# Projecting the prompt's queries in transposed form, and moving their token factors into the group norm's epsilon

## What is computed

```
h = rmsnorm(x);  u, q, k, v, g = split(h @ w_in)            # 1024 -> 5 x 512
pool_out = pool_mix(u)                                       # trailing means, a 128x128 product per group
qh, kh = rope(q), rope(k) * 128 ** -0.5                      # 4 heads of 128
# retention, chunks of 128 tokens, per head, gamma a constant of the head
scores = (qc @ kc.T) * decay_mat                             # gamma^(i-j) for i >= j
o = scores @ vc + (qc * gamma^(i+1)) @ s
s = s * gamma^128 + (kc * gamma^(127-j)).T @ vc
o = (o - mean(o)) * rsqrt(var(o) + GN_EPS) * gn_g            # group norm over a head's 128 values
x = x + concat(pool_out, silu(g) * o) @ w_out
```

## Time and profile before

| what | value |
|---|---|
| three runs | 836.44, 837.12 (median), 838.64 us |
| the profiled execution | 837.1 us |
| its span on the core | 835.1 us |
| mean granted TensorE clock | 0.995 of full speed |
| PE busy | 814.2 us, 97% of the span |
| DVE busy | 599.4 us, 72% |
| ACT busy | 483.6 us, 58% |
| POOL busy | 315.4 us, 38% |

### The profile page before, as it was taken

How to read it: one execution, slowest core, us unless ns; L and a number is a source line. 1 busy time by engine, 2 the same in 40 slices (tenths; PEclk the granted TensorE clock), 3 DMA queues, 4 the chain that set the end, 5 groups by cost and what they waited for, 6 DMA issues and landing times.

```text
span 835.1 us, 11973 instructions
## 1 busy us (share of the span) xinstructions
PE 814.2 (97%) x4104; PEld 656.6 (79%) x4104; DVE 599.4 (72%) x957; ACT 483.6 (58%) x824; POOL 315.4 (38%) x205
## 2 busy tenths in 40 slices
PE   9999999999999999999899999999999999999994
PEld 6887788888867888888488788888878578888861
DVE  5444654645689999999744454656647899999986
ACT  5533342612478888887653433353333898888874
POOL 0016991301041345664100199803101423665540
PEclk9999999999999999999999999999999999999998
DMA  9832223223939999998753222322278599999968
GB/s 323 271 109 76 72 57 98 91 70 137 411 128 361 388 355 377 397 368 300 255 185 92 85 76 64 87 64 78 78 263 346 179 417 360 383 378 391 344 219 280
DMA packets 57422, 188.17 MB, mean 225 GB/s; under 512 B 10877, under 2 KB 11645, under 8 KB 49163
## 3 DMA queue, kind: packets, MB, share of 16 engines
q1 hardware_dynamic: 44314, 156.55, 52.2%
q0 software_dynamic: 10368, 23.09, 7.4%
q10 hardware_dynamic: 2688, 7.88, 2.5%
HBM read 173.00 MB, written 29.39 MB: 242 GB/s over the span
## 4 chain that ended last, share of the span: by engine, by line
PE 71%; DVE 16%; DMA 5%; issue 4%; ACT 2%; DVEq 0%; ACTq 0%; POOLq 0%
PE ps L464 14%; PE ps L468 11%; PE ps L467 11%; PE ps L1414 5%; PE ps L1416 5%; PE ps L1415 5%; DVE gul L2110 4%; DVE dnl L2115 3%; PE ps L466 3%; PE ps L1422 2%; DVE hgTl L2126 2%; DMA y_d<-y,rowidx 2%; PE ps L1665 2%; DMA back<-y_d 1%; PE ps L1605 1%
## 5 line engine op out<-in xcount | busy, mean ns | idle before, releaser
L464 PE MATMUL ps<-wh,hT 128*128 128x512 f32 x472 | 189.4, 401 | 0.8 <-DVE wl L2101 0.4
L866 POOL DMA_INDIRECT y_d<-y,rowidx x32 | 116.4, 3638 | 124.1 <-DVE y L2135 124.1
L2110 DVE TENSOR_TENSOR gul<-wgu,eh 128x1024 fp32r<-128x1024 f32 x128 | 150.4, 1215 | 0.5 <-ACT eh L1105 0.5
L468 PE MATMUL ps<-wh,lT 128*128 128x512 f32 x377 | 147.2, 390 | 0.0
L467 PE MATMUL ps<-wl,hT 128*128 128x512 f32 x377 | 147.0, 390 | 0.0
L1105 ACT ACTIVATE eh<-wgu 128x1024 fp32r<-128x1024 f32 x128 | 128.4, 1058 | 3.7 <-PE ps L1416 3.7
L2101 DVE SCALAR_TENSOR_TENSOR wl<-raw,gcol,wh 128x512 fp32r<-128x512 f32 x80 | 75.3, 946 | 67.9 <-ACT wh L1078 67.8
L464 PEld LDWEIGHTS ps<-wh,hT 128*128 128x128 f32 x472 | 88.8, 188 | 18.8 <-issue 1.7
L1414 PE MATMUL ps<-eh,hgTh 128*128 128x512 f32 x240 | 96.4, 401 | 0.4 <-issue 0.4
L1416 PE MATMUL ps<-eh,hgTl 128*128 128x512 f32 x240 | 93.8, 391 | 0.0
L1415 PE MATMUL ps<-gul,hgTh 128*128 128x512 f32 x240 | 93.5, 390 | 0.0
(11 more groups left out here) (259 smaller groups left out, 1555.6 us busy)
## 6 DMA issues: line engine op xcount, KB each, us to landing
wgu<-in_gate_up SPq DMA_DIRECT2D x64, 1024.0 KB, 12.6
wdn<-in_w_down SPq DMA_DIRECT2D x64, 512.0 KB, 12.2
raw<-in_w_in SPq DMA_DIRECT2D x79, 256.0 KB, 2.7
raw<-in_w_out SPq DMA_DIRECT2D x32, 256.0 KB, 3.0
back<-y_d SPq DMA_DIRECT2D x16, 512.0 KB, 5.9
s<-in_state_ret POOLq DMA_DIRECT2D x8, 512.0 KB, 4.3
xn_d<-xf ACTq DMA_DIRECT2D x8, 512.0 KB, 6.2
x_in<-in_x_cols SPq DMA_DIRECT2D x8, 288.0 KB, 5.0
```

The lines of the kernel that those rows point to most:

```text
L464: pe.matmul(out, both, w_h, start=first, stop=False)
L468: return pe.matmul(out, l[:, t * P:(t + 1) * P], w_h, start=False, stop=final)
L866: pool.indirect_dma_start(out=y_d, out_offset=bass.IndirectOffsetOnAxis(ap=rowidx[:, 1, e:e + 1], axis=0), in_=y[s][:, :], in_offset=None, ...
L2110: ve.tensor_tensor(gu_pair(gul, gul3, e, s, p), gu_pair(wgu, wgu3, e, s, p), gu_split(e, p)[:, :].bitcast(F32), ALU.subtract).then_inc(glo, 1)
```

## The change

- For the q block, and the four prompt tiles, the operands change places: a 128-column slice of `wh` or `wl` is stationary and all 512 prompt tokens stream, so a bank then holds one head of q, already transposed (128 dimensions on the partitions, 512 tokens along them). The number of matmuls and their widths stay.
- The bank is copied out without `rstd`. A token's factor, and the decay of its row, scale a whole row of the output, and the group norm takes that out again when its epsilon is divided by the factor's square: `gneps` (a table) times `msq` (the mean square plus epsilon), added to the variance by one more small DVE operation (`gnv`). `q_decay` and `qdT` go; the decay mask becomes one of the key alone.
- POOL rotates q by head (`rotate_turned`): four linked operations over 512 elements, the two in the middle on 64 partitions each, reading one half of the partitions and writing the other. All four heads are rotated before the first k tile.
- `qk_t` transposes only k of the prompt tiles, ACT copies only `kT`. The sample tile keeps the old way; its scores are 64x64.
- `T_AT` and `S_AT` move by one step for tiles 0 and 1.

```diff
-T_AT, S_AT, O_AT = (28, 30, 34, 37), (29, 31, 35, 38), (33, 36, 39)
+T_AT, S_AT, O_AT = (29, 31, 34, 37), (30, 32, 35, 38), (33, 36, 39)
...
+            def rotate_turned(L, h):
+
+                z_there(pool, L, 1, h)
+                v = z[:, h, OFFS["q"], :]
+                cs, sn = c("cosT"), c("sinT")
+                link(pool.tensor_tensor(turnA[:, :], v, cs, ALU.mult))
+                link(pool.tensor_tensor(turnB[0:HALF, :], v[HALF:P, :], sn[HALF:P, :], ALU.mult))
+                link(pool.tensor_tensor(turnB[HALF:P, :], v[0:HALF, :], sn[0:HALF, :], ALU.mult))
+                link(pool.tensor_tensor(v, turnA[:, :], turnB[:, :], ALU.add))
...
-                rotate(L, 0, 0)
-                rotate(L, 1, 0)
+                rotate_turned(L, 0)
+                rotate_turned(L, 1)
                 window(L, 3)
-                rotate(L, 2, 0)
-                for t in range(3):
+                rotate_turned(L, 2)
+                rotate_turned(L, 3)
+                for t in range(LAST):
                     rotate(L, t, 1)
-                for t in (3, LAST):
-                    rotate(L, t, 0)
-                    rotate(L, t, 1)
+                rotate(L, LAST, 0)
+                rotate(L, LAST, 1)
...
-                sc.activation(qT[:, :, :], heads(ps[B_Q][:, :]), ACT.Copy).then_inc(qk_ev, 1)
+                if t == LAST:
+                    sc.activation(qT[:, :, :], heads(ps[B_Q][:, :]), ACT.Copy).then_inc(qk_ev, 1)
...
-                last = tile_mm(pe, ps[m % ZB][:, :], hT[:, k, :], lT[:, k, :], wh[S % SPL][:, :], wl[S % SPL][:, :], t, k == 0, k == KC - 1)
+                if g == 1 and t < LAST:
+                    own = slice(t * P, (t + 1) * P)
+                    last = three(ps[m % ZB][:, :], wh[S % SPL][:, own], wl[S % SPL][:, own], hT[:, k, 0:SEQ], lT[:, k, 0:SEQ], k == 0, k == KC - 1)
+                else:
+                    last = tile_mm(pe, ps[m % ZB][:, :], hT[:, k, :], lT[:, k, :], wh[S % SPL][:, :], wl[S % SPL][:, :], t, k == 0, k == KC - 1)
...
-                for h in range(NH):
-                    pe.transpose(ps[B_Q][:, h * P:(h + 1) * P], zq(t, "q")[:, h * P:(h + 1) * P], ident)
+                if t == LAST:
+                    for h in range(NH):
+                        pe.transpose(ps[B_Q][:, h * P:(h + 1) * P], zq(t, "q")[:, h * P:(h + 1) * P], ident)
...
-                pe.wait_ge(qd_done, T + 1)
...
-                last.then_inc(gn_st, 1)
+                link(last)
+                ve.scalar_tensor_tensor(out=gnv[:, :], in0=c("gneps", 2)[:, int(t == LAST), :], scalar=msq[:, t:t + 1], in1=mv[:, :, 1],
+                                        op0=ALU.mult, op1=ALU.add).then_inc(gn_st, 1)
...
-                    if s - 3 in T_AT:
-                        if s - 3 == T_AT[0]:
-                            ve.wait_ge(upool_st, 32 * (L + 1))
-                        q_decay(L, T_AT.index(s - 3))
...
-                q_decay(L, LAST)
```

More of the change, by code:

```diff
@@ L107, in constant_tables @@
         "decay": np.stack([decay(P), decay(DECS)], 1),
-        "qdec": np.stack([qdecay(P), qdecay(DECS)], 1),
+        "cosT": np.concatenate([np.cos(ang)[:, :LAST]] * 2, 2).transpose(2, 1, 0),
+        "sinT": np.concatenate([np.sin(ang)[:, :LAST], -np.sin(ang)[:, :LAST]], 2).transpose(2, 1, 0),
+        "gneps": np.stack([row_eps(P), row_eps(DECS)], 1),
         "kdec": np.stack([kdecay(P)] + [kdecay_sample(0 if L + 1 < NL else LATE) for L in range(NL)], 1),
@@ L273, in build @@
         gnrs = tile("gnrs", [P, NH])
+        gnv = tile("gnv", [P, NH])
+        msq = tile("msq", [P, NT])
         eps = tile("eps", [P, 2])
@@ L300, in build @@
         ropB = tile("ropB", [P, NH, 2, HALF], off=s0_at[1] + 2048)
+        turnA = tile("turnA", [P, SEQ], off=s0_at[1])
+        turnB = tile("turnB", [P, SEQ], off=s0_at[1] + 2048)
         on = [heads_tile(f"on{t}", d_at + 2048 * t if t < LAST else r12 + 10 * 1024) for t in range(NT)]
@@ L381, in heads, with q_turned, keys_there @@
             return ap.rearrange("p (h d) -> p h d", h=NH)
+        def q_turned(h, t):
+            return qT[:, h, 0:NSAMP] if t == LAST else z[:, h, OFFS["q"], t * P:(t + 1) * P]
+        def keys_there(L, t):
+            return (NT + 1) * L + (NT + 1 if t == LAST else t + 1)
         def over(ap, n, dim=1):
@@ L1089, in z_evac @@
                     func = ACT.Silu if g == 4 and t < LAST else ACT.Copy
-                    sc.activation(dst, ps[m % ZB][:, :], func, scale=rstd[:, t:t + 1]).then_inc(z_part if t == LAST else zfree[m % ZB], 1)
+                    by = 1.0 if g == 1 and t < LAST else rstd[:, t:t + 1]
+                    sc.activation(dst, ps[m % ZB][:, :], func, scale=by).then_inc(z_part if t == LAST else zfree[m % ZB], 1)
             def gate_last(L):
@@ L1207, in group_root @@
                 sc.wait_ge(gn_st, NT * L + t + 1)
-                sc.activation(gnrt[:, :], mv[:, :, 1], ACT.Sqrt, bias=eps[:, 1:2], scale=1.0).then_inc(gn_rt, 1)
+                sc.activation(gnrt[:, :], gnv[:, :], ACT.Sqrt).then_inc(gn_rt, 1)
             def first_hi(k):
@@ L1624, in scores @@
             def scores(L, t):
-                T = NT * L + t
-                pe.wait_ge(qk_ev, 2 * T + 2)
-                pe.wait_ge(qd_done, T + 1)
+                pe.wait_ge(qk_ev, keys_there(L, t))
+                n = tokens(t)
                 for h in range(NH):
-                    last = pe.matmul(ps[B_SC][:, h * P:(h + 1) * P], kT[:, h, :], qT[:, h, :], start=True, stop=True)
+                    last = pe.matmul(ps[B_SC][0:n, h * P:h * P + n], kT[:, h, 0:n], q_turned(h, t), start=True, stop=True)
                 last.then_inc(sc_mm, 1)
@@ L1646, in outputs @@
                     if t:
-                        last = pe.matmul(out, qdT[t % 2][:, h, :], st[:, h, :], start=False, stop=True)
+                        last = pe.matmul(out, q_turned(h, t), st[:, h, :], start=False, stop=True)
                 last.then_inc(o_mm, 1)
@@ L1664, in sample_head @@
                 for b in range(DECB):
-                    last = pe.matmul(out[:, b * DECS:(b + 1) * DECS], s0[h][:, b, :], qdT[0][:, h, b * DECS:(b + 1) * DECS],
+                    last = pe.matmul(out[:, b * DECS:(b + 1) * DECS], s0[h][:, b, :], qT[:, h, b * DECS:(b + 1) * DECS],
                                      start=False, stop=(b == DECB - 1))
@@ L2020, in mix_scale @@
                 ve.wait_ge(rms_done, 6 * L + 1)
+                ve.tensor_tensor(msq[:, 0:LAST], rms[:, 0:LAST], rms[:, 0:LAST], ALU.mult)
                 ve.reciprocal(rstd[:, :], rms[:, :]).then_inc(rstd_done, 1)
@@ L2163, in _ @@
             ve.memset(still[:, :], 0.0).then_inc(still_set, 1)
+            ve.memset(msq[:, LAST:NT], 1.0)
             ve.memset(x[NSAMP:P, LAST, :], 0.0).then_inc(ready0, 1)
@@ L2169, in z_evac @@
                     dst = unat[:, t, :] if g == 0 else z[:, t, g - 1, :]
-                    ve.tensor_scalar(dst, ps[m % ZB][:, :], rstd[:, t:t + 1], None, ALU.mult).then_inc(zfree[m % ZB], 1)
+                    if g == 1:
+                        ve.tensor_copy(dst, ps[m % ZB][:, :]).then_inc(zfree[m % ZB], 1)
+                    else:
+                        ve.tensor_scalar(dst, ps[m % ZB][:, :], rstd[:, t:t + 1], None, ALU.mult).then_inc(zfree[m % ZB], 1)
             def z_last(L, g):
@@ L2221, in late_sum @@
                                         op0=ALU.mult, op1=ALU.add).then_inc(comb, 1)
[L2223 to L2229, removed]
             def score_decay(L, t):
```

10 lines of the change are left out of this document (4 added, 6 removed).

## The result

The changed kernel takes 838.63 us (median of 22 runs, 837.59 to 841.28), the kernel before 836.58 us on the same chips (22 runs, 835.76 to 839.24). The ratio is 1.002, with a 95% interval of 1.0013 to 1.0028: some 2 us slower. The profiled execution took 838.6 us (span 836.7, before 835.1).

The account below looks back on a forecast made before the run. PE, working 814.2 of 835.1 us, was taken as the bound. The terms, -3.5 (transposes) + 3.1 (pooling product) + 0.4 (first k tile) = 0.0, gave 837.1 us, range 833.4 to 840.8.

Parts of the forecast that it names:

- The transposes: On PE, q transposes of four prompt tiles in two layers go: 8 x 0.44 = 3.5 us gained.
- something else holds PE at those steps: Rival: at steps 28 to 37 removing the transposes would not free their time; dismissed, without a numerical chance.
- Exchanged matmuls and the sample's scores: On PE, exchanged q matmuls taken as 0 (up to 1 us lost), 64x64 sample scores as 0 (up to 0.8 gained).
- The turned rotations: On POOL before window 3, two rotations take 12.5 us: 11.0 undisturbed plus 1.5 from DVE collisions; before 9.55.
- The upper bound of 3.6 us for window 3: POOL's window 3 at most 3.6 us later, each collision at 0.66 and one at the window's head; 2.9 forecast.
- The pooling product: PE's product of group 3, awaiting DVE's dT behind window 3: with group 2, 3.1 us new waits, bounds 0 and 7.
- The first k tile: Ready from POOL at 111.0, asked for by PE at 110.9: a tie, 0.2 us per layer, 0 to 1.2 for the range.
- They cost nothing unless that cover goes, and then some 0.3 us each: DVE's small gnv with its link, ten times, and msq, twice: free while PE asks a step or more later.
- the normalised tiles at the end of the mixer: Listed sign of a wrong prediction: new PE waits for these tiles; no size given.
- the rotations hardly grow: Faster rival: two turned rotations take at most 11.0 us, window 3 late by 1.5; 833.6 us; faster case 0.28.
- The pooling product waits longer: Slower rival: group 3's pool_d takes 4.9 us, dT after 98.4 in layer 0; 841.6 us; slower case 0.22.
- The clock: Rival that a 2 us wait lowers PE's clock; expected to stay at 1.00, given no chance of its own.

Follow-up runs that it names:

- experiment 1: Kernel before, with the two 256-element operations of POOL's rotation done twice for q tiles 0 and 1; 841.66 us, ratio 1.0056 to the kernel before.
- experiment 4: Changed kernel, with heads 1 and 3 rotated by DVE in steps 19 and 20 instead of POOL; 834.95 us, ratio 0.9967 to the kernel before.
- one_rot: Changed kernel, with POOL's window 3 behind one turned rotation instead of two; 847.97 us, ratio 1.0127 to the kernel before.
- one_rot_k_later: Changed kernel, window 3 behind one turned rotation and first k tiles one step later; 842.39 us, ratio 1.0063 to the kernel before.
- one_rot_k_later_last_act: Changed kernel, window 3 behind one turned rotation, first k tiles a step later, sample tile's epsilon added by ACT; 841.32 us, ratio 1.0049 to before.

## Why the prediction was right or wrong

- **The transposes** were worth 3.5 in the sum, 3.2 measured alone and 3.2 on PE in that trace. Right in kind, and by the trace 0.3 too large. The rival that something else holds PE at those steps is out with it.
- **Exchanged matmuls and the sample's scores** at 0: right (390 to 398 ns for each; in layer 0 the sample's scores take 0.61 in place of 0.89 us, and 0.1 of that is left where the state product begins behind them).
- **The turned rotations** at 12.5 us: 12.5 measured. The operations on 64 partitions take 1.29 to 1.30 us undisturbed, as assumed, and the collisions come to the 1.5 us that were estimated. The upper bound of 3.6 us for window 3 does not come out of its own parts (1.5 + 4 x 0.66 is 4.1); nothing hung on it.
- **The pooling product** at 3.1 us of new waits: 3.0 measured (3.2, of which 0.2 were there before). Window 3 is later by 3.4 - 0.24 = 3.1 (2.9 forecast), `pool_d` takes 3.15 (3.2 forecast); experiment 1 makes the same wait from the rotations alone, and experiment 4 takes it away.
- **The first k tile** was called a tie, 0.4 us: 0.9 measured. The mechanism was right, the term too small, since k0 was done at 111.48 (111.0 forecast; 0.24 of the difference is the later start of this trace).
- **The step that failed** is the one on `gnv`: "They cost nothing unless that cover goes, and then some 0.3 us each". The cover was looked for in DVE's free share and in PE asking a step later. In the sample tile's chain there is no such cover: DVE's `wl` had gone ahead of POOL's `vb` by 0.39 us, and an operation that took 0.69 us lost that place. The price in the trace is 0.54 us of PE in each layer, paid not by `gnv` but by the `wl` that it put second. The prediction named "the normalised tiles at the end of the mixer" as a place where it might go wrong, and priced it at nothing. The other terms were right in mechanism and off in size, the k tile by 0.5 us and the transposes by 0.3.

By these terms the sum is -3.2 + 3.0 + 0.9 + 1.1 = 1.8, against 2.05 between the medians and 1.7 on PE in the two mixers. It should not be read as closer than it is: the 1.1 is shown on PE, and in the whole time by medians only (above), and before's own profile runs part of the routing of layer 0 at the lower clock (granted 0.67 from 235 to 239 us, after 1.00), which takes about 0.8 us from the difference of the two traces. Without the 1.1 the terms leave 0.7, below the interval of 1.1 to 2.3 us. How much of the mixer's end reaches the whole time, and what varies behind it (the routing's wait is 0.9 to 1.8 us in these traces, the last read-back's 1.0 to 2.8), stays open.

Of the rivals, "the rotations hardly grow" was wrong from the start of the new stretch. "The pooling product waits longer" did not come: `dT` was done at 97.34, not after 98.4. The clock, given no chance at a wait of 1.6 us, did stay at 1.00 there, and fell in the kernels with longer waits.

## What to carry to other kernels

Work moved off the busiest engine is worth only what the next one in the chain can take on: here POOL paid back in waits all that PE had gained, and a version that gives half of POOL's new work to an engine that idles at that time keeps most of it (833.6 to 835.0 us). An operation's own duration is not its price where two engines hold each other up: look at which of the two was first before, by how much, and who waits for the loser. Before an operation is moved up in a queue, look at when its input is made: in the kernel before window 3 started at 84.02 us behind two rotations, and its input came no earlier (83.89 in one_rot, where POOL idled for it).

## What the runs showed of the hardware that I had not expected

- An operation of 128x4 elements on DVE took 0.22 us at best and 0.69 us beside POOL's 128x1024; the `wl` after it took 0.68 us when it began 0.39 us ahead of POOL's operation and 2.38 us when it began 0.36 us behind it.
- One and the same stop of PE, 2.4 us for the first k tile of layer 0, was followed by a granted clock of 0.62 in the next 4 us in one execution (one_rot_k_later) and of 1.00 in another (one_rot_k_later_last_act). In layer 1 it fell behind the same stop in both, to 0.58 and 0.73. The stops of 1.6 us left it at 1.00 in the kernel after; in the 4 us in which PE starts again after the stops of 5.0 us (one_rot) it was 0.73 and 0.57.
